# Square sums moved from VectorE to ScalarE, modulation units redistributed over three stages, and one silu taken from a broadcast load

## The reference, cut to what matters

```
shift, scale, gate = split(silu(c) @ ada_w + ada_b)
h = rms_norm(x, norm_g) * (1 + scale) + shift
u, v, z = split(h @ w_in, 3)
v = rms_norm(gelu(v), sgu_g)              # needs the sum of squares of each row of gelu(v)
mixed = einsum(tril(w_s), v) + b_s        # per group, along the tokens
y = gelu(u) * mixed * silu(z)
x = x + gate * (y @ w_out)
```

## Time and profile before

| | |
|---|---|
| time of three runs | 1593.43 us median (1592.54 to 1594.86) |
| time of the profiled execution | 1596.76 us |
| its span, first to last instruction | 1595.0 us |
| granted TensorE clock, mean | 0.976 of full |
| PE / DVE / ACT / POOL busy | 1508.3 / 936.7 / 592.7 / 199.2 us |
| share of PE in the chain that ended last | 83% |
| share of "DMA ada_v<-in_ada" in that chain | 3% |

### The profile page before, as it was taken

How to read it: one execution, slowest core, us unless ns; L and a number is a source line. 1 busy time by engine, 2 the same in 40 slices (tenths; PEclk the granted TensorE clock), 3 DMA queues, 4 the chain that set the end, 5 groups by cost and what they waited for, 6 DMA issues and landing times.

```text
span 1595.0 us, 19527 instructions
## 1 busy us (share of the span) xinstructions
PE 1508.3 (95%) x7344; PEld 1203.1 (75%) x7344; DVE 936.7 (59%) x1397; ACT 592.7 (37%) x835; POOL 199.2 (12%) x73
## 2 busy tenths in 40 slices
PE   5799999999889999999999799999897999999999
PEld 3798788888668788888877566776565888888887
DVE  5888777764485466666664537767755344333243
ACT  4322323231265454445532545545443323211131
POOL 0000110000010322222223122213103000000000
PEclk9989999999989999999999799999998999999999
DMA  9688454555312112111102012111112232222222
GB/s 364 250 320 326 171 197 159 185 199 203 139 53 97 63 57 76 54 53 53 54 29 104 27 53 74 36 50 53 37 43 80 79 105 80 104 106 79 106 71 87
DMA packets 33052, 178.40 MB, mean 112 GB/s; under 512 B 3810, under 2 KB 4066, under 8 KB 18404
## 3 DMA queue, kind: packets, MB, share of 16 engines
q1 hardware_dynamic: 32116, 175.22, 30.2%
q10 hardware_dynamic: 880, 2.41, 0.5%
HBM read 175.52 MB, written 2.10 MB: 111 GB/s over the span
## 4 chain that ended last, share of the span: by engine, by line
PE 83%; DVE 10%; DMA 3%; ACT 2%; issue 2%; DVEq 0%; SPq 0%; ACTq 0%
PE acc L1313 71%; PE ada L1313 4%; DMA ada_v<-in_ada 3%; PE norm L1313 3%; PE turn L1313 2%; PE turn L1516 1%; DVE ada_v L816 1%; PE turn L1628 1%; DVE s L1206 1%; DVE ada_up L816 1%; DVE hk_lo L816 1%; DVE w_lo L823 1%; DVE h_lo L816 1%; DVE hx L816 1%; DVE s L1223 0%
## 5 line engine op out<-in xcount | busy, mean ns | idle before, releaser
L1313 PE MATMUL acc<-h_hi,w_hi 128*128 128x512 f32 x992 | 407.1, 410 | 11.8 <-DVE h_lo L816 8.6
L1313 PE MATMUL acc<-h_lo,w_hi 128*128 128x512 f32 x992 | 390.0, 393 | 0.0
L1313 PE MATMUL acc<-h_hi,w_lo 128*128 128x512 f32 x992 | 389.8, 393 | 0.0
L467 ACT ACTIVATE w_hi<-w_raw 128x2048 fp32r<-128x2048 f32 (+1 forms) x106 | 200.6, 1893 | 140.4 <-PE acc L1313 122.8
L1313 PEld LDWEIGHTS acc<-h_hi,w_hi 128*128 128x128 f32 x992 | 188.4, 190 | 65.0 <-issue 16.6
L1313 PEld LDWEIGHTS acc<-h_lo,w_hi 128*128 128x128 f32 x992 | 188.6, 190 | 43.8 <-issue 7.2
L1313 PEld LDWEIGHTS acc<-h_hi,w_lo 128*128 128x128 f32 x992 | 188.3, 190 | 40.2
L415 POOL TENSOR_TENSOR w_lo<-w_raw,w_hi 128x2048 fp32r<-128x2048 f32 x32 | 147.0, 4592 | 563.3 <-ACT w_hi L467 563.3
L823 DVE TENSOR_TENSOR w_lo<-w_raw,w_hi 128x2048 fp32r<-128x2048 f32 (+1 forms) x74 | 168.4, 2276 | 77.6 <-ACT w_hi L467 77.5
L1313 PE MATMUL acc<-w_hi,h_hi 128*128 128x256 f32 x320 | 94.7, 296 | 14.3 <-DVE w_lo L823 14.3
L816 DVE SCALAR_TENSOR_TENSOR x<-acc,mods,x 128x512 f32<-128x512 f32 (+1 forms) x40 | 33.2, 832 | 127.5 <-PE acc L1313 127.4
(11 more groups left out here) (214 smaller groups left out, 2513.8 us busy)
## 6 DMA issues: line engine op xcount, KB each, us to landing
w_raw<-in_weights SPq DMA_DIRECT2D x102, 1024.0 KB, 4.7
ada_v<-in_ada SPq DMA_DIRECT2D x48, 512.0 KB, 7.0
ada_raw<-in_ada SPq DMA_DIRECT2D x48, 512.0 KB, 5.6
ada_up<-in_ada_first SPq DMA_DIRECT2D x8, 1024.0 KB, 18.1
w_raw<-in_weights SPq DMA_DIRECT2D x4, 768.0 KB, 4.1
x<-in_x SPq DMA_DIRECT2D x2, 1024.0 KB, 8.9
w_first<-in_weights SPq DMA_DIRECT2D x2, 1024.0 KB, 14.4
out<-x SPq DMA_DIRECT2D x8, 256.0 KB, 2.0
```

The lines of the kernel that those rows point to most:

```text
L467: nc.scalar.activation(w_hi[par][:, 0:used], w_raw[par][:, 0:used], ACT.Copy).then_inc(hi_done, 1)
L1313: return nc.tensor.matmul(out, lhsT, rhs, start=start, stop=stop)
```

## The change

The change does five things.

1. UNITS_V, UNITS_UZ, UNITS_OUT go from 6, 2, 2 to 4, 2, 4. The total stays at 96. A v chunk now uses each of the four `ada_v` slots once. In the out stage a ring of four tiles `ada_out` is used: the two of `ada_raw`, the place of `ws_t` (free after the last mixing matmul) and that of `csil[0]`.
2. The sums of squares of v are made by ACT (`v_chunk`): after each gelu of half a chunk, two Square activations of 128 x 256 with an accumulated sum.
3. SP loads weight chunks 2 and 3 one behind the other before any `ada_v` tile, and DVE's and ACT's first chunks are written out so that `w_hi` and `w_lo` of chunk 3 are made between the units of chunk 0 and of chunk 1.
4. silu(c_2): c_2 is loaded already spread over the partitions by a DMA from the ACT queue, and ACT takes its silu in place during the v stage; only c goes through PE and PSUM at the start.
5. In the out stage DVE does two of a chunk's four units ahead of `to_lo` and two behind it. The bias of the first 48 units is added in the middle of the u/z stage, between two loops.

The diff, cut to its core:

```diff
-UNITS_V, UNITS_UZ, UNITS_OUT = 6, 2, 2
+UNITS_V, UNITS_UZ, UNITS_OUT = 4, 2, 4
...
+    ada_out = [at(f"ada_out{s}", [P, DM], off) for s, off in enumerate((off_ada, off_ada + 4 * KB, big + 64 * KB, big + 68 * KB))]
...
+            def ada_out_loads(u, par):
+                for e in range(UNITS_OUT):
+                    k = 2 * UNITS_OUT * u + UNITS_OUT * par + e + FIRST_OUT_UNIT
+                    src = ada_row(k)
+                    if isinstance(u, int) and par == 0:
+                        sp.wait_ge(ada_done, FIRST_OUT_UNIT - 1 + min(e, 1))
+                        if e == 2:
+                            sp.wait_ge(mix_done, AT)
+                    else:
+                        sp.wait_ge(ada_done, k - 3)
+                    sp.dma_start(ada_out[e][:, :], src).then_inc(ada_out_loaded[e], 16)
...
             for par in range(2):
                 load(1, par)
+            for par in range(2):
                 ada_v_loads(0, par)
...
+            act.dma_start(csil[1][:, :], d["c_2"][0].partition_broadcast(P)).then_inc(c2_loaded, 16)
-            for n in range(4):
+            for n in range(2):
                 act.wait_ge(c_spread_in, n + 1)
...
+            def v_chunk(u, par, first=False):
+                n = 2 * u + par - W_V
+                for hb in range(2):
+                    act.wait_ge(mm_done, 4 * u + 2 * par + hb + 1)
...
+                    act.wait_ge(v_gelu_done, 4 * u + 2 * par + hb + 1)
+                    ge(act, v_sums_done, 2 * n + hb - 1)
+                    for t in range(2 * hb, 2 * hb + 2):
+                        act_v = nc.scalar.activation(v_sq[:, t, :], v[:, t, bass.ds(256 * n, 256)], ACT.Square,
+                                                     accum_out=v_sums[:, t, bass.ds(n, 1)])
+                    act_v.then_inc(v_sums_done, 1)
+            for par in range(2):
+                v_chunk(0, par, True)
+            to_hi(1, 1)
+            act.wait_ge(c2_loaded, 16)
+            nc.scalar.activation(csil[1][:, :], csil[1][:, :], ACT.Silu).then_inc(csil_ready, 1)
+            v_chunk(1, 0)
+            to_hi(2, 0)
+            v_chunk(1, 1)
+            with act.Fori(2, W_UZ // 2) as u:
+                for par in range(2):
+                    to_hi(*next_chunk(u, par))
+                    v_chunk(u, par)
...
                 for par in range(2):
                     m = 2 * u - W_OUTA + par
+                    ada_out_units(m, (0, 1))
                     to_lo(*next_chunk(u, par))
-                    ada(m + AT)
+                    ada_out_units(m, (2, 3))
                     update_x(m, G[2 * par][:, :], GATE_A, 4 * u + 2 * par + 2, 2)
```

More of the change, by code:

```diff
@@ L350, in ada_v_loads, with ada_loads @@
                         sp.wait_ge(ada_done, k - 3)
-                    sp.dma_start(ada_v[slot][:, :], src).then_inc(ada_v_loaded[slot], 16)
+                    sp.dma_start(ada_v[e][:, :], src).then_inc(ada_v_loaded[e], 16)
+            def ada_loads(u, par):
+                for e in range(UNITS_UZ):
+                    k = 2 * UNITS_UZ * u + UNITS_UZ * par + e + FIRST_UZ_UNIT
+                    src = ada_row(k)
+                    if not (isinstance(u, int) and k < FIRST_UZ_UNIT + 2):
+                        sp.wait_ge(ada_done, k - 1)
+                    sp.dma_start(ada_raw[e][:, :], src).then_inc(ada_loaded[e], 16)
+            def ada_out_loads(u, par):
+                for e in range(UNITS_OUT):
+                    k = 2 * UNITS_OUT * u + UNITS_OUT * par + e + FIRST_OUT_UNIT
+                    src = ada_row(k)
+                    if isinstance(u, int) and par == 0:
[5 more added lines that the diff above has]
+                    sp.dma_start(ada_out[e][:, :], src).then_inc(ada_out_loaded[e], 16)
             def ada_up_load(kt):
@@ L385, in _ @@
                     load(u, par)
[L386 to L388 removed]
+                    ada_loads(u - W_UZ // 2 - 1, par)
+            for par in range(2):
+                load(W_OUTA // 2 + 1, par)
+                ada_out_loads(0, par)
+            with sp.Fori(W_OUTA // 2 + 2, W_KV // 2 + 1) as u:
                 for par in range(2):
                     load(u, par)
[L391 to L392 removed]
+                    ada_out_loads(u - W_OUTA // 2 - 1, par)
             with sp.Fori(W_KV // 2 + 1, W_Q2 // 2) as u:
@@ L828, in unit, with ada_v_units, ada_units, ada_out_units @@
                     accum_out=mods[:, bass.ds(k + FIRST_MODS, 1)]).then_inc(ada_done, 1)
-            def ada_v_unit(u, par, e):
-                slot = (UNITS_V * par + e) % 4
-                dve.wait_ge(ada_v_loaded[slot], 16 * (2 * UNITS_V // 4 * u + (UNITS_V * par + e) // 4 + 1))
-                unit(2 * UNITS_V * u + UNITS_V * par + e, ada_v[slot], 0)
-            def ada(i):
-                for e in range(2):
-                    dve.wait_ge(ada_loaded[e], 16 * (i + 1))
-                    unit(2 * i + e + FIRST_UZ_UNIT, ada_raw[e], 1)
+            def ada_v_units(u, par):
+                for e in range(UNITS_V):
+                    dve.wait_ge(ada_v_loaded[e], 16 * (2 * u + par + 1))
+                    unit(2 * UNITS_V * u + UNITS_V * par + e, ada_v[e], 0)
+            def ada_units(j, cond):
+                for e in range(UNITS_UZ):
+                    dve.wait_ge(ada_loaded[e], 16 * (j + 1))
+                    unit(UNITS_UZ * j + e + FIRST_UZ_UNIT, ada_raw[e], cond)
+            def ada_out_units(m, es):
+                for e in es:
+                    dve.wait_ge(ada_out_loaded[e], 16 * (m + 1))
+                    unit(UNITS_OUT * m + e + FIRST_OUT_UNIT, ada_out[e], 1)
             def add_bias(lo, hi):
```

100 lines of the change are left out of this document (41 added, 59 removed).

## The result

The changed kernel takes 1568.26 us in the median of four runs (1567.09 to 1568.71), the kernel before 1593.57 beside it (1592.54 to 1594.86): ratio 0.984, 95% interval 0.9823 to 0.9857. That is 25.3 us, where 27.4 were forecast; 1568.26 lies in the range of 1561 to 1574, 2.3 above the 1566 named. The profiled execution took 1568.05 (span 1566.3), against the forecast of 1569.2 (1567.4) made from the profiled execution of before.

What follows compares the result with a forecast made beforehand. PE, busy 95%, carries most of the chain, and the v stage is slightly transfer-bound. Removing 24.8 us of waits and lower clock plus 2.8 at the start, 27.6 with costs of 0, gave 1566 us, range 1561 to 1574.

Steps and rivals of the forecast that it cites:

- Items 1 to 4: PE's waits and lower clock from chunk 3 through chunks 8 and 9: 13.1, 2.6, 1.7 and 7.4 us removed, 24.8 together.
- Item 5: Start: c_2's silus and their two matmuls leave the path to the first norm, gaining 2.8 us, bounds 0 and 2.9.
- The costs added: Squares on ACT, later `w_lo` of chunks 3 and 4, moved out-stage units: all covered by margins, taken as 0 us.
- Rival B: v stage: chunk 4's `w_lo` comes late behind eight units and `ws_t`, up to 5.2 us lost, 1571; chance 0.12.
- The loop of the out stage: `w_lo` frees `w_raw`, chunk and two tiles load, unit, next `w_lo`: 10.6 to 11.8 us against PE's 11.165; loss taken 0.
- rival E: Out stage: late tiles lengthen the loop until the kernel is slower than before, 1599 with a 17 us loop; chance 0.03.
- 6L - 68.8: Out stage loss in us by chunk 31 for loop length L: nothing at 10.6, 2.0 at 11.8.
- Which median: Profiled run 3.3 us above median: profile's own gives 1565.8, v stage transfers 1569.1; 1566 taken.
- Rivals C and D: C: start gains nothing, 1568.8, chance 0.08; D: v stage stays bound by its tile ring, 1578, chance 0.05.
- A to E: The five cases; A, all waits go and none comes, 1566, chance 0.72; the others 0.12, 0.08, 0.05, 0.03.

Runs made afterwards that it cites:

- before_again: The kernel before, unchanged, run and traced a second time: 1593.44 us, ratio 1.0004.
- late_lo3: The changed kernel with chunk 3's `w_lo` put back behind eight units and the `ws_t` product instead of behind four units: 1571.02 us, ratio 0.9862.
- four_ahead: The changed kernel with four `ada_out` units ahead of `w_lo` in the out stage instead of two: 1585.47 us, ratio 0.9949.
- three_ahead: The changed kernel with three `ada_out` units ahead of `w_lo` in the out stage instead of two: 1576.20 us, ratio 0.9882.
- squares_back: The changed kernel with the squares of v again on DVE, behind the four units of each chunk: 1568.97 us, ratio 0.9844.
- lo_first: The changed kernel with `w_lo` ahead of all four units in the out stage: 1565.67 us, run again 1567.60 beside the changed kernel's 1567.97.
- start_only: The kernel before with only the new start, c_2 by broadcast load and c alone through PE: 1591.07 us, ratio 0.9984.
- six_units: The changed kernel without its distribution of units: 6/2/2 and the old rings kept: 1584.16 us, ratio 0.9937.
- dist_only: The kernel before with only the distribution 4/2/4 and both rings; squares on DVE, old order and old start: 1576.60 us, ratio 0.9895.

## Why the prediction was right, and what was off

**Items 1 to 4, the waits in and behind the v stage: right.** Forecast 24.8. The traces give 28.83 - 3.93 = 24.9 between chunk 2's start and chunk 24's, all of it before chunk 10. Nothing took the place of these waits. That the two agree within 0.1 holds for the trace out of which the items were read: against before_again the same stretch gains 279.9 - 258.1 = 21.8, so some 3 us of the items were that one execution's. The last v gelu is at 124.42 (forecast near 125.5), chunk 10 at 147.65 (near 149).

**Item 5, the start: a little too small.** Forecast 2.8 with an upper bound of 2.9, measured 3.9 at chunk 2 in this pair of traces. DVE's adds begin at 11.53, 3.1 earlier; the bound kept the old time of `lam_prod`, which ends 0.13 earlier now, and its last accumulator read overlaps with the adds. PE's four matmuls for the norm then take 3.48 us instead of 3.75, at a granted clock of 1.00 in both; why isn't known. So `x_n` and the first matmul on h are 3.4 earlier (23.36 for 26.78). The last 0.5 is the lower clock behind the first matmul on h, which lasts 4.4 us now instead of 5.7 (rows in the last section); it lasts 3.9 to 6.1 in other traces, whatever the start. The second silu runs at 7.07 and not at 8.17, since PE's spreading of c waits for one load and no longer for two, and the first square of x is at 9.34 where 10.1 was forecast; but this isn't on the path, as the adds wait for `lam_prod`. So part of the 3.9 is this pair's luck: chunk 2 starts at 57.95 to 58.75 in the three traces with the old start and at 54.77 to 56.00 in the ten with the new one, 3.1 apart in the means.

**The costs added: right at 0, on thinner margins than forecast.** Chunk 3's `w_lo` ends at 62.8 and PE takes it up at 66.5: 3.7 of margin, 3.4 forecast. Chunk 4's ends at 76.5 and PE takes it up at 78.0: 1.5 instead of 2.2. The reason given for the 0 at this place failed. The prediction had the queue nearly empty there and the tiles landing in 3.3 us; the queue was full (395 GB/s, DMA share 0.98, in the window above), and the tiles issued from 60 to 80 us landed in 4.8 to 6.7. Three of the four tiles ahead of chunk 4's `w_lo` came late, 0.8 us together, and the cover of 2.2 took that up. So the term was right by its cover, not by the light traffic. Rival B did not happen, and late_lo3 shows that it is a real price, 3 us of wait and 1.7 behind it.

**The loop of the out stage (rival E's mechanism): right, and confirmed in size.** Forecast 10.6 to 11.8 us, measured 10.95, once 12.4. four_ahead and three_ahead show the loss by 6L - 68.8 within 1 to 2 us, and within 0.2 once the late first `w_lo` is counted.

The windows of 11.5 and 11.7 us with 395 and 422 GB/s, all of it loads from HBM, and the loop of 10.95 us bear on the rate at which loads can come. The Trainium skill, page "DMA: Bandwidth & Descriptors", section "Bandwidth", says that for loads from HBM a limit of about 358 GB/s binds; its condition, that both cores of a pair are streaming, stands in the same section, and the prediction left it out. The windows are above that, and the loop was nearer to the 10.6 worked out with 426 than to the estimate of 11.5 made from the page: the measurement decides against it here. This program ran on one core alone, and for that case the Trainium skill, page "HBM Reference", section "Specifications (TRN2)", gives about 425 GB/s; by this rule, the trace agrees.

**Which median: the step that was most off.** The prediction weighed whether the first profiled execution's 3.3 us above the median were the profile's own (1565.8) or sat in the v stage's transfers (1569.1), and took 1566. before_again shows the latter: of the 4.5 us between the two spans 3.8 are ahead of chunk 24. The changed kernel has no wait there that could stretch, so its profiled execution (1568.05) lies on its median (1568.26), and the plain gain is 25.3, not 28.7. With item 5 at its measured size (3.9 in the pair, 3.1 in the mean) that way of reckoning gives 1568.0 to 1568.8. The argument used, that three runs agreed within 2.3, was no evidence: 31 runs spread over 7.8.

**Rivals C and D.** Neither happened. In the changed kernel the start comes through whole: in seven traces whose chunk 2 starts at 54.77 to 56.00 (the two of the changed kernel, squares_back, four_ahead, three_ahead and the two of lo_first), chunk 24 follows 258.0 to 258.1 us behind in each. For the kernel before, start_only gives 1.5 to 2.5 where PE starts 3 earlier, but its interval of 1.1 to 4.0 doesn't tell these apart.

Two small sums of the prediction don't close. The chances of A to E add up to 1.00 without the 0.01 for none, and B on top of 1569.1 is 1574.3, just outside of 1574. Neither changes the forecast.

**What is shown and what isn't.** Shown by runs: the distribution is worth 16.7, the rest together 8.4 to 10.0, the squares on ACT nothing measurable, two units instead of four ahead of `w_lo` about 17. How the rest splits can be read from marks in single traces only: six_units starts chunk 2 3.1 us before before_again and takes 4.4 less from there to chunk 24, and the changed kernel takes 5.6 less there than dist_only (258.1 for 263.7). So about 3 are the start and 4 to 6 the new order at the beginning of the v stage with the squares on ACT, which these runs change together; late_lo3, which takes back the place of one `w_lo` alone, loses 4.7 of them. That transfers swallow a part of start_only's gain is argued from its waits, not shown.

## What to carry to other kernels

Where a wait's length is set by how many transfers stand ahead of one load in an in-order list, reordering moves the wait to the next chunk (six_units), and fewer transfers in that stage take it away. When work is moved to a later stage, write the loop that frees a slot, loads it and uses it, and set its length against PE's time for a step: with one unit more ahead of `w_lo` this change gives up a third of its gain, with two more, two thirds. If one profiled execution lies off the median of a kernel whose transfers bind a stage, take a second one before a difference of two per mille is put down to the profile.

## What the runs showed of the hardware

A stop costs more than its length, and the extra grows little with it. Chunk 3 takes 11.51 us in the changed kernel (66.52 to 78.03). Behind a stop of 2.96 us it took 1.6 more (late_lo3), behind 4.07 us 1.4 more (dist_only), and behind 13.06 us 2.3 more (before). In before the first 5.2 us behind the stop had a granted clock of 0.52.

Behind the out stage of four_ahead and three_ahead the next stretch, to the second block, took 446.3 and 446.5 us, 2.7 to 2.9 longer than the 443.5 to 443.7 of the other traces. The traces show where: the last `w_lo` stands ahead of DVE's update of x (it starts at 417.40, 0.2 before PE is through, in four_ahead), so the square of the new x is 1.6 us later behind PE's end and PE waits 2.41 for it instead of 0.80; and the two matmuls behind that wait take 2.07 us instead of 1.13.

The lower clock lasts differently long in the same place. Behind the first matmul on h it is 0.50 of full (1.2 GHz) for 5.7 us in the kernel before and for 4.4 in the changed one (windows, columns as above):

```profile
28.40:34.10 5.70, 5.68 (x14) 4.48 (x14) 5.56 (x14) 2.02 (x3) 0.00 (x0) 0.50 1.00 424
```

```profile
25.00:29.40 4.40, 4.40 (x11) 3.51 (x11) 4.33 (x10) 2.01 (x3) 0.00 (x0) 0.50 1.00 425
```

The first is of before, the second of after; PE ran the same matmuls after the same idle time of 5.17. It isn't the edit. In other traces the matmuls in this place take 1.06 us for two instead of 0.59 for 6.1 us with the new start (squares_back, 25.45 to 31.6) and for 3.9 with the old one (dist_only, 28.36 to 32.3). So it varies between executions; what sets it isn't settled.

A stage that nothing changed differs between executions. The attention of the second block takes 339.6 us in before's trace and 335.6 in late_lo3's, with the same instructions:

```profile
874.70:1214.30 339.60, 318.67 (x1537) 223.98 (x1536) 209.56 (x384) 160.97 (x312) 71.86 (x19) 0.96 0.14 50
```

```profile
850.70:1186.30 335.60, 313.67 (x1537) 221.10 (x1536) 209.22 (x384) 160.79 (x312) 71.50 (x19) 0.98 0.15 51
```

The granted clock is 0.96 and 0.98 (the column before the last two). In thirteen traces this stage lies between 335.6 and 339.6, with no relation to the edits that I can see. A single total can't tell 3 us here, and marks inside the trace can: late_lo3's traced execution took 1568.72, as the changed kernel's, and hid that chunk 24 started 4.9 us later.

The one long loop of the out stage (12.4 us) came at the same place, the third loop, in both traces of the changed kernel, behind an `ada_out` tile 1.4 us late each time (353.15 and 353.73), and in those of four_ahead and three_ahead too. What it collides with there wasn't found.
